# Second attention: queries split into rounded and low parts in one-head pieces of 128 tokens

## The reference, cut to what matters

```python
def attention_mixer(h_lat, h_ctx, w_qkv, q_norm, k_norm, w_o, rope, with_ctx_out):
    q_l = apply_axial_rope(queries(h_lat), rope)
    k_all = jnp.concatenate([k_c, k_l], axis=2)
    v_all = jnp.concatenate([v_c, v_l], axis=2)
    ...
    o_blocks = lax.map(lambda qb: gqa_attend(qb, k_all, v_all), q_blocks)   # 512 latent queries, 768 keys
    ...
    o_c = gqa_attend(queries(h_ctx), k_c, v_c)                              # 256 context queries, 256 keys
```

## Time and profile before

| | |
|---|---|
| median of 3 runs | 3610.65 us (3608.27 to 3615.75) |
| the profiled execution | 3610.93 us |
| its span | 3609.1 us |
| PE busy | 3254.8 us, 90% |
| DVE busy | 1550.9 us, 43% |
| ACT busy | 1124.5 us, 31% |
| POOL busy | 535.9 us, 15% |
| mean granted TensorE clock | 0.942 of full |
| second attention | about 1749 to 2010 us |

### The profile page before, as it was taken

The page is one execution under the profiler, slowest core; times in us unless marked ns, Lnnn a source line. Parts: engine busy times, 40 slices in busy tenths (PEclk is TensorE's granted clock), DMA queues, the critical chain, the costliest instruction groups (busy, mean ns, idle before and its releaser), DMA issues. The chain is left out here.

```text
span 3609.1 us, 48582 instructions
## 1 busy us (share of the span) xinstructions
PE 3254.8 (90%) x19154; PEld 2431.0 (67%) x19154; DVE 1550.9 (43%) x2410; ACT 1124.5 (31%) x1679; POOL 535.9 (15%) x394
## 2 busy tenths in 40 slices
PE   7997957999998899988787989999998999899998
PEld 5665611576466687867566778886556888748877
DVE  5644178243224666222655332220006887723332
ACT  4213153142113333233555332220004544422321
POOL 0000022000103343250122220000004322100001
PEclk9998978999999999989798889999997999889999
DMA  3564110121230222211000011111112111112222
GB/s 132 201 250 169 59 38 0 70 95 47 94 128 24 93 94 79 89 66 65 1 1 1 24 47 70 70 47 48 50 68 75 55 69 71 51 67 93 97 84 88
DMA packets 30566, 267.90 MB, mean 74 GB/s; under 512 B 2864, under 2 KB 5296, under 8 KB 10160
## 3 DMA queue, kind: packets, MB, share of 16 engines
q1 hardware_dynamic: 30384, 265.36, 20.0%
HBM read 261.15 MB, written 4.19 MB: 74 GB/s over the span
## 5 line engine op out<-in xcount | busy, mean ns | idle before, releaser
L632 PE MATMUL banks<-normed_high,weights_high 128*128 128x512 f32 (+1 forms) x2264 | 842.0, 379 | 84.6 <-DVEq L455 47.5
L632 PE MATMUL banks<-normed_low,weights_high 128*128 128x512 f32 (+1 forms) x2264 | 831.4, 375 | 0.0
L632 PEld LDWEIGHTS banks<-normed_high,weights_high 128*128 128x128 f32 x2264 | 437.3, 193 | 192.3 <-ACT weights_high L542 41.5
L632 PE MATMUL banks<-normed_high,weights_low 128*128 128x512 f32 (+1 forms) x2264 | 544.5, 371 | 0.0
L263 DVE TENSOR_TENSOR weights_low<-ring,weights_high 128x1024 fp32r<-128x1024 f32 (+1 forms) x194 | 269.5, 1389 | 607.3 <-ACTq L555 539.2
L632 PEld LDWEIGHTS banks<-normed_low,weights_high 128*128 128x128 f32 x2264 | 438.9, 194 | 73.1 <-issue 1.2
L632 PEld LDWEIGHTS banks<-normed_high,weights_low 128*128 128x128 f32 x2264 | 405.2, 191 | 73.7
L553 ACT ACTIVATE weights_high<-ring 128x1024 fp32r<-128x1024 f32 (+1 forms) x226 | 260.9, 1154 | 618.1 <-PE banks L632 452.5
L587 POOL TENSOR_TENSOR latent_total<-latent_total,latent_square 128x512 f32<-128x512 f32 x42 | 77.1, 1836 | 1441.9 <-ACTq L530 1441.9
L632 PE MATMUL banks<-ffn_hidden,ring 128*128 128x256 f32 (+1 forms) x704 | 227.3, 486 | 1.1 <-PEq L154 1.1
L2830 PE MATMUL banks<-normed_high,hg_weights_high 128*128 128x512 f32 (+1 forms) x512 | 190.1, 371 | 15.1 <-DVEq L455 15.1
(11 more groups left out here) (539 smaller groups left out, 4787.9 us busy)
## 6 DMA issues: line engine op xcount, KB each, us to landing
ring<-in_ffn_up SPq DMA_DIRECT2D x33, 2048.0 KB, 7.5
ring<-in_ada SPq DMA_DIRECT2D x48, 1024.0 KB, 6.4
ring<-in_ffn_down SPq DMA_DIRECT2D x24, 1408.0 KB, 5.9
ring<-in_hgrn SPq DMA_DIRECT2D x16, 1536.0 KB, 6.4
ring<-in_gates SPq DMA_DIRECT2D x6, 2048.0 KB, 8.1
ring<-in_wo SPq DMA_DIRECT2D x6, 2048.0 KB, 8.0
ring<-in_w_rw SPq DMA_DIRECT2D x5, 1536.0 KB, 7.5
ring<-in_branch SPq DMA_DIRECT2D x3, 2048.0 KB, 7.8
```

What stands on the lines that cost most here:

```text
L632: mm = pe.matmul(ps[:, 0:y.shape[-1]], w, y, start=(not sweep and kk == 0 and n == 0), stop=(sweep != 0 and kk == kt - 1 and n == len(pair ...
```

## The change

The split is made unit by unit. `part(u)` is one ACT instruction and one DVE instruction of 64 partitions by 128 columns, and signals `queries_rounded` and `queries_parted` straight from the instruction, with no wait for its own end and no separate increment. `pa_queries` becomes a ring of eight such pieces. Four pieces are made ahead of the loop, and pass u of both loops makes the piece of unit u + 4, if there is one. PE waits for its piece in each unit. ACT waits, before it writes into a place of the ring, for the scores of the unit eight earlier.

```diff
--- before.py
+++ after.py
@@ -2331,15 +2331,17 @@
     project()
 
 
+QUERIES_AHEAD = 4
+
+
 def pair_attention(k, Q, KH, KL, V, H, scale):
 
 
     pairs = [(t, LAT, T) for t in range(DT)] + [(t, CTX_, CTX) for t in range(DT)]
     groups = [(j, qt) for j, (t, cols, keys) in enumerate(pairs) for qt in range((cols.stop - cols.start) // P)]
     units = [(g, p) for g in range(len(groups)) for p in range(2)]
-    first_group, last_group = {}, {}
+    last_group = {}
     for g, (j, qt) in enumerate(groups):
-        first_group.setdefault(j, g)
         last_group[j] = g
     n_units, n_groups, n_pairs = len(units), len(groups), len(pairs)
     scored, maxed, exped, inverted, normed, turned, kept_s, kept_v, multiplied, high_taken, low_taken = (
@@ -2348,7 +2350,7 @@
                              "output_high_taken", "products_taken"))
     rounded, parted = k.count("queries_rounded"), k.count("queries_parted")
     with ExitStack() as s:
-        QS = k.sb("pa_queries", [P, 2, 2, L], s, F32R)
+        QS = k.sb("pa_queries", [P, 2 * QUERIES_AHEAD, P], s, F32R)
         PB = k.sb("pa_probs", [P, 3, T], s)
         PT = k.sb("pa_turned", [P, 2, 2, T // P, P], s)
         MX, NM, SM, RS = (k.sb("pa_" + x, [P, 4], s) for x in ("max", "bias", "sum", "inverse"))
@@ -2360,6 +2362,10 @@
             t, cols, keys = pairs[j]
             return g, p, j, qt, t, cols, keys
 
+        def queries(u):
+            g, p, j, qt, t, cols, keys = of(u)
+            return Q[rows(p), t, cols.start + qt * P:cols.start + qt * P + P]
+
         def split_at(keys):
 
             n = keys // P
@@ -2373,12 +2379,11 @@
             def _(pe):
                 def score(u):
                     g, p, j, qt, t, cols, keys = of(u)
-                    if qt == 0 and p == 0:
-                        pe.wait_ge(parted.sem, parted.at(j + 1))
+                    pe.wait_ge(parted.sem, parted.at(u + 1))
                     if u >= 2:
                         pe.wait_ge(exped.sem, exped.at(u - 1))
                     b, kv = 2 * (u % 2), 2 * (t // 4) + p
-                    q = QS[:, j % 2, p, qt * P:qt * P + P]
+                    q = QS[:, u % (2 * QUERIES_AHEAD), :]
                     for c in range(0, keys, 512):
                         w = min(512, keys - c)
                         pe.matmul(k.PS[b + c // 512][:, 0:w], q, KH[:, kv, c:c + w], start=True, stop=False)
@@ -2427,16 +2432,11 @@
             def _(v):
                 e = k.engine(v, "vector_steps", ends)
 
-                def part(j):
-
-                    t, cols, keys = pairs[j]
-                    w = cols.stop - cols.start
-                    v.wait_ge(rounded.sem, rounded.at(j + 1))
-                    for p in range(2):
-                        v.tensor_tensor(QS[rows(1 - p), j % 2, p, 0:w], Q[rows(p), t, cols],
-                                        QS[rows(p), j % 2, p, 0:w].bitcast(F32), ALU.subtract).then_inc(e.sem, e.tick())
-                    v.wait_ge(e.sem, e.now())
-                    v.sem_inc(parted.sem, 1)
+                def part(u):
+                    p, x = units[u][1], u % (2 * QUERIES_AHEAD)
+                    v.wait_ge(rounded.sem, rounded.at(u + 1))
+                    v.tensor_tensor(QS[rows(1 - p), x, :], queries(u), QS[rows(p), x, :].bitcast(F32),
+                                    ALU.subtract).then_inc(parted.sem, 1)
 
                 def maximum(u):
                     keys = of(u)[6]
@@ -2466,8 +2466,8 @@
                     v.wait_ge(high_taken.sem, high_taken.at(j + 1))
                     v.tensor_tensor(lo, k.PS[6 + j % 2][:, 0:cols.stop - cols.start], hi.bitcast(F32),
                                     ALU.subtract).then_inc(low_taken.sem, 1)
-                part(0)
-                part(1)
+                for u in range(QUERIES_AHEAD):
+                    part(u)
                 maximum(0)
                 for u in range(n_units + 6):
                     if u + 1 < n_units:
@@ -2476,10 +2476,8 @@
                         invert(u)
                     if 1 <= u <= n_units:
                         keep(u - 1)
-                    if u < n_units and units[u] == (first_group[groups[units[u][0]][0]], 1):
-                        j = groups[units[u][0]][0]
-                        if 1 <= j and j + 1 < n_pairs:
-                            part(j + 1)
+                    if u + QUERIES_AHEAD < n_units:
+                        part(u + QUERIES_AHEAD)
                     if u >= 5 and (u - 5) % 2 == 0 and (u - 5) // 2 < n_groups:
                         g = (u - 5) // 2
                         if g == last_group[groups[g][0]]:
@@ -2499,17 +2497,11 @@
             def _(a):
                 e = k.engine(a, "scalar_steps", ends)
 
-                def part(j):
-
-                    t, cols, keys = pairs[j]
-                    w = cols.stop - cols.start
-                    if j >= 2:
-
-                        a.wait_ge(scored.sem, scored.at(2 * last_group[j - 2] + 2))
-                    for p in range(2):
-                        a.activation(QS[rows(p), j % 2, p, 0:w], Q[rows(p), t, cols], ACT.Copy).then_inc(e.sem, e.tick())
-                    a.wait_ge(e.sem, e.now())
-                    a.sem_inc(rounded.sem, 1)
+                def part(u):
+                    p, x = units[u][1], u % (2 * QUERIES_AHEAD)
+                    if u >= 2 * QUERIES_AHEAD:
+                        a.wait_ge(scored.sem, scored.at(u - 2 * QUERIES_AHEAD + 1))
+                    a.activation(QS[rows(p), x, :], queries(u), ACT.Copy).then_inc(rounded.sem, 1)
 
                 def exponentials(u):
                     keys = of(u)[6]
@@ -2556,7 +2546,7 @@
             ends.update(scores_ready=n_units, maximum_ready=n_units, exps_ready=n_units, sums_inverted=n_units,
                         probs_ready=n_units, probs_turned=n_units, turned_kept_scalar=n_units, turned_kept_vector=n_units,
                         group_multiplied=n_groups, output_high_taken=n_pairs,
-                        products_taken=n_pairs, queries_rounded=n_pairs, queries_parted=n_pairs)
+                        products_taken=n_pairs, queries_rounded=n_units, queries_parted=n_units)
 
 
 def heads_norm_rope(k, tiles, KH, KL):
```

## The result

| | before | after |
|---|---|---|
| median | 3610.65 us (3608.27 to 3615.75, 3 runs; a fourth took 4577.98 and is left out) | 3655.14 us (3651.26 to 3662.68, 4 runs) |
| profiled execution | 3610.93 us | 3655.47 us |
| its span | 3609.1 us | 3653.7 us |
| mean granted TensorE clock | 0.942 | 0.940 |

The ratio of after to before is 1.0126, with a 95% interval of 1.0111 to 1.0141: slower by 1.3%, some 45 us (3655.14 - 3610.65 = 44.5).

A forecast was written before the change was run, and what follows sets the result against it. PE was taken as near the bound, with holes at each pair's rounding; after the change a loop between ACT and DVE would bind. Stretches sum to +39.7 us, plus 5 for the clock, +44.7 on 3610.93: 3655 us, range 3640 to 3668.

The forecast's parts named there:

- The loop closed in every unit: Second attention: DVE's piece waits for ACT's of the same pass, ACT's exponentials for DVE's maximum, in all but four units.
- A latent unit, 3.37 us: Latent part, units 0 to 63: steps from one bias to the next on DVE and ACT sum to 3.37 us.
- A context unit, 2.10 us: Context part, units 64 to 95: steps round the ACT and DVE loop sum to 2.10 us.
- Output of a pair, 0.90 and 0.42 us: Once a pair, ACT's high part and DVE's low part lengthen the loop: 0.90 us latent, 0.42 us context.
- The head, -2.2 us: Start of the stage: PE needs only one piece of each engine, so it starts 2.2 us earlier.
- The clock, +5 us: PE idles about 2.1 us a group; slowed multiplies could cost 0 to 29 us over 32 groups, 5 taken.
- rival 1: TensorE's clock drops with PE's short holes: 3679 us if every group is slow, about 3665 if half; chance 0.19.
- The sum: Second attention: the stretches between roundings together +39.7 us, with 5 us for the clock +44.7.
- Units 57 to 65: Latent stretch: 20.95 us before, 27.9 after (8 x 3.37 + 0.90), +6.9.
- units 89 to 92: Last context stretch: plain steps of 1.6 us before become 2.10, +1.5 us.
- The holes of before: Latent part before the change: all the missing 5.5 us per eight units sit at the one rounding in each pair.
- Rival 2, a wait that is not felt: ACT reaches its piece before DVE needs it, rounding stalls vanish, PE bounds again: 3561 us; chance 0.04.

The follow-up runs named there:

- run 1: The changed kernel with ACT's piece made one pass ahead of DVE's (ACT five units ahead, DVE four): 3589.56 us, ratio 0.9928.
- run 2: The changed kernel with ACT's piece put first in the pass, ahead of the exponentials: 3586.77 us, ratio 0.9926.
- run 3: The kernel before (whole pairs) with ACT's rounding one pass earlier than DVE's subtraction: 3588.88 us, ratio 0.9925.
- run 8: Run 3's whole pairs with DVE's low part a pass later: 3579.20 us, ratio 0.9910; also the changed kernel with pieces six units ahead: 3657.00 us.
- run 7: Run 6's open kernel with DVE's subtraction moved ahead of the reciprocal: 3556.21 us, ratio 0.9853.
- run 4: The changed kernel with the pieces of two units made together in every second pass on both engines: 3609.17 us, ratio 0.9986.
- run 6: DVE's low part of a pair's output a pass later: on run 2's kernel (open) 3569.79 us, on the changed kernel (closed) 3651.41 us.

## Why the prediction was right, point by point

The forecast was 3655 us and the median is 3655.14; the mechanism is the one forecast. The exact hit is partly luck, since terms were off on both sides, and its reading of the kernel before was in part wrong, at a place on which the sum does not rest:

- *The loop closed in every unit.* Right: 92 waits of DVE for ACT's piece, 1.57 to 1.77 us in latent units, even intervals, and runs 1 and 2 take the loss away without touching size or number of the instructions.
- *A latent unit, 3.37 us.* Low by 0.1: the intervals are 3.43 and 3.50, for lack of two details. The piece starts 0.49 or 0.62 us behind the copy (1827.65 - 1827.03), where I had one row with 0.49; and when it starts at 0.49, the maximum starts 0.31 behind the subtraction (1824.68 - 1824.37), not 0.20. Over 64 units that is 6 us.
- *A context unit, 2.10 us.* Low by 0.09: 2.15 and 2.22.
- *Output of a pair, 0.90 and 0.42 us.* Low: 1.06 and 0.58 (4.53 and 2.76 against the mean of their neighbours).
- *The head, -2.2 us.* Right: PE's first score is 0.68 us after ACT's first rounding, where it was 2.88.
- *The clock, +5 us.* Too high. All but two of the latent intervals, 3.79 and 3.83 us, are undisturbed, which makes some 0.7 us. The clock did fall now and then (9 of 32 latent multiplies took 2.0 to 2.8 us and not 1.53), but the loop hardly felt it, and rival 1, whose price needs every group or half of them slow and felt, did not come. With PE busy 147.08 of 212 us, 69%, the granted clock of the latent stretch is 0.92. It is 0.90 before, but that difference lies ahead of 1760, at the head of the stage: from 1760 on it is 0.92 in both kernels (the second pair of rows, before and after). In the context stretch it is 0.66 with a loop that does not feel it:

```profile
1750.00:1962.00 212.00, 147.08 (x1268) 125.19 (x1267) 108.59 (x303) 112.56 (x243) 53.58 (x59) 0.92 0.00 1
1962.00:2052.00 90.00, 59.87 (x393) 45.24 (x391) 45.35 (x189) 46.52 (x152) 19.95 (x37) 0.66 0.00 1
...
1760.00:1946.00 186.00, 153.59 (x1375) 130.93 (x1374) 110.17 (x277) 109.04 (x213) 57.20 (x64) 0.92 0.00 1
1760.00:1962.00 202.00, 142.45 (x1242) 121.64 (x1241) 103.61 (x288) 106.58 (x230) 50.85 (x56) 0.92 0.00 1
```

- *The sum.* +44.7 forecast for the stage, and 47.2 measured; the start of the stage, 3.1 us earlier in the profiled execution, brought the span back to +44.6. By the bias intervals of both traces the terms came out as below. The undersized steps of the loop are in units 9 to 57 and 65 to 89. Units 57 to 65 came out lower than forecast: the last intervals there are already 2.90 and 2.54 us. At units 89 to 92 the sum took a plain context step for all three units of before, though the stall behind the rounding at unit 89 lies in that stretch (3.50 + 0.80 + 2.56 us, against 7.14 now), so +1.5 should have been near 0. The end of the stage was not in the sum.

| stretch | forecast | measured |
|---|---|---|
| head | -2.2 | -2.2 |
| first two units | 0 | +0.3 |
| units 1 to 9 | +7.6 | +8.3 |
| units 9 to 57 | +21.8 | +27.8 |
| units 57 to 65 | +6.9 | +4.6 |
| units 65 to 89 | +4.1 | +6.9 |
| units 89 to 92 | +1.5 | +0.3 |
| end of the stage | 0 | +1.3 |
| clock | +5.0 | some 0.7, in the rows above |
| together | +44.7 | +47.2 |

- *The holes of before.* The prediction put all the missing 5.5 us of eight latent units at the rounding and said that elsewhere DVE runs free of ACT. Neither holds. DVE also waits for ACT's high part in each pair (0.76 us in the earlier trace rows; 5.5 us for the eight latent pairs and 3.5 for the context ones). The bias intervals of before, from one rounding to the next, are 5.73, 1.45, 4.51, 3.15, 1.58, 3.04, 1.60 and 3.03 us, so about half of what is missing lies at the third and fourth, around the output of the pair. Giving ACT a pass of lead takes 2.1 to 2.7 of the 5.5 us (run 3), the low part a pass later 0.8 to 1.3 more (run 8), and about 2.1 stay with whole pairs. The sum was not harmed, because its lengths of before are measured ones.
- *Rival 2, a wait that is not felt.* It fell for the change as written. Its condition, a lead of ACT over DVE, was the right one, though the prediction held that only a whole pass of lead would do: run 1 gives that, and run 2 opens the loop within the same pass, by the order alone. But its price, 50 us less than before, was far too good for them (26 less): it took every hole of before for the roundings', and left out DVE's wait for the high parts and the long subtractions beside POOL. With both gone it is 54 less (run 7).

The number of small pieces was not what cost the 45 us: the 96 small copies are 302 ns, as the line through two rows gave, and run 4 shows the same 96 at a cost of nothing against the kernel before. Their length counts only where they lie on the closed loop.

## What to carry to other kernels

When a step is cut finer and moved into each pass of two engines' loops, look at what stands ahead of it on the engine that makes it: if that waits for the engine that uses it, every pass becomes one trip round both engines, however far ahead the result is made for a third. Give the maker a pass of lead, or put its step ahead of what waits; here both took the 45 us back and 26 more (runs 1 and 2). In the timeline such a loop shows as two engines that take turns, each idle while the other works, with the engine that used to be the bound idle beside them.

## What the runs showed of the hardware that was not expected

- A DVE subtraction with both inputs in SBUF takes 286 ns by itself and up to 792 ns (run 6) when POOL's scaling of a tile in SBUF is running, and then ends 0.12 to 0.27 us behind POOL's instruction; a 128x768 maximum that reads PSUM is 0.94 to 0.96 us long with or without POOL beside it (run 7). The Trainium skill has the rule ("SBUF — State Buffer", section "SBUF: two separate sides", on the port pair that DVE and GpSimd share): the pair is locked for a whole instruction by whichever starts first, and a DVE instruction with two SBUF inputs needs it when the GpSimd instruction reads SBUF, as this scaling does. The traces agree, and the prediction did not use it; in the changed kernel the wait for ACT's piece happened to push every subtraction behind POOL (286 ns in all 92).
- The granted clock of TensorE stayed mostly at its higher level in the changed kernel with PE idle for 1.9 to 2.9 us in each group: 0.92 in the mean from 1760 to 1962, with PE busy 142.45 of 202 us. It was also 0.92 from 1760 to 1946 before, with PE busy 153.59 of 186 us and a hole of 4.13 us at the roundings. The longer idle time in all and the missing of the long holes came together, and neither was tried by itself. The lower level also comes without a long hole: it is there at the multiply at 1775.31, which takes 2.83 us, and from 1757 to it PE has no hole over 1.91 us.
